# Two softmax attentions of a four-block network: where transposition, values and logits stand in a software-pipelined step

## The reference

```python
def fox_mixer(q, k, v, f_logit):          # 8 heads, in blocks of 128 queries
    ...
    logits = (einsum('bqhd,bshd->bhqs', qb, k) * scale
              + cq[..., None] - cum_k[:, :, None, :])
    p = masked_softmax(logits, causal)
    return einsum('bhqs,bshd->bqhd', p, v)

def dsa_mixer(q, ckv, k_rope, q_idx, k_idx, w_idx, w_uk, w_uv):   # 8 heads
    ...
    score = einsum('bqhs,bqh->bqs', relu(einsum('bqhd,bsd->bqhs', qi, k_idx)), wi)
    _, idx = top_k(score, n_keep)          # 128 keys for each query
    logits = (einsum('bqhr,bqkr->bqhk', qa, c_sel)
              + einsum('bqhe,bqke->bqhk', qr, kr_sel)) * scale
    p = masked_softmax(logits, valid)
    return einsum('bqhk,bqkr->bqhr', p, c_sel)
```

## Time and profile before

| | |
|---|---|
| median of 3 runs | 2276.22 us (2272.16 to 2279.46) |
| profiled execution: time, span | 2279.5 us, 2278.2 us |
| TensorE busy | 2219.5 us, 97% of the span |
| VectorE busy | 1348.9 us, 59% |
| ScalarE busy | 560.6 us, 25% |
| GpSimd busy | 192.0 us, 8% |
| mean granted TensorE clock | 0.995 of full speed |
| fox attention | from 131.8 to 258.2 us of the span |
| dsa attention | from 259.3 to 314.5 us |

### The profile page before, as it was taken

How to read it: one execution, slowest core, us unless ns; L and a number is a source line. 1 busy time by engine, 2 the same in 40 slices (tenths; PEclk the granted TensorE clock), 3 DMA queues, 4 the chain that set the end, 5 groups by cost and what they waited for, 6 DMA issues and landing times.

```text
span 2278.2 us, 29581 instructions
## 1 busy us (share of the span) xinstructions
PE 2219.5 (97%) x10992; PEld 1589.9 (70%) x10992; DVE 1348.9 (59%) x3440; ACT 560.6 (25%) x1421; POOL 192.0 (8%) x207
## 2 busy tenths in 40 slices
PE   9999999999999999999999999999999999999988
PEld 7776578888888885558888888888857534333333
DVE  6777757666566667876665666767786522222224
ACT  2223431101001206772110000333572111111110
POOL 0013430000000002330000000000020011111100
PEclk9999999999999999999999999999999999999999
DMA  5211032232222320002232222232205899999997
GB/s 211 75 57 47 13 123 77 90 93 85 82 93 91 116 74 19 1 1 67 82 93 90 78 92 93 75 103 64 66 9 232 326 422 422 424 422 424 424 423 305
DMA packets 60207, 346.54 MB, mean 152 GB/s; under 512 B 9248, under 2 KB 10144, under 8 KB 42208
## 3 DMA queue, kind: packets, MB, share of 16 engines
q1 hardware_dynamic: 55360, 335.03, 39.6%
q0 software_dynamic: 3840, 6.46, 0.8%
q10 hardware_dynamic: 864, 3.15, 0.3%
HBM read 337.59 MB, written 17.30 MB: 156 GB/s over the span
## 4 chain that ended last, share of the span: by engine, by line
PE 87%; DMA 7%; DVE 4%; ACT 1%; issue 1%; SPq 0%; DVEq 0%; POOLq 0%; ACTq 0%
PE bank L632 30%; PE bank L638 8%; PE bank L645 8%; PE bank L653 8%; DMA places<-in_experts 7%; PE bank L3038 6%; PE bank L3046 3%; PE bank L621 3%; PE bank L1098 2%; PE bank L1083 2%; PE bank L1110 2%; PE bank L2998 1%; PE bank L727 1%; PE bank L3011 1%; PE bank L1305 1%
## 5 line engine op out<-in xcount | busy, mean ns | idle before, releaser
L3038 PE MATMUL bank<-places,xT 128*64 128x512 f32 x824 | 183.8, 594 | 13.5 <-DMA places<-in_experts 13.4
L3245 DVE TENSOR_SCALAR square<-bank,mt 128x256 f32<-128x256 f32 x32 | 15.5, 483 | 287.2 <-ACT rope L3150 287.2
L3038 PEld LDWEIGHTS bank<-places,xT 128*64 128x64 f32 x824 | 59.4, 137 | 132.3 <-issue 118.0
L1959 DVE TENSOR_TENSOR third<-first,bank 128x256 f32<-128x256 f32 x106 | 44.7, 421 | 151.0 <-PE bank L632 150.3
L632 PE MATMUL bank<-u,ring 128*128 128x256 f32 x540 | 130.3, 381 | 1.1 <-DVE y_ab L1993 1.1
L632 PE MATMUL bank<-h,ring 128*128 128x256 f32 x512 | 121.0, 379 | 0.0
L632 PE MATMUL bank<-h_sums,w_sum 128*128 128x256 f32 x512 | 120.9, 379 | 0.0
L632 PEld LDWEIGHTS bank<-u,ring 128*128 128x128 f32 x540 | 101.2, 190 | 17.8 <-issue 3.3
L632 PE MATMUL bank<-u_mlp_sums,w_sum 128*128 128x256 f32 x480 | 113.4, 379 | 0.0
L632 PE MATMUL bank<-u_mlp,ring 128*128 128x256 f32 x480 | 113.4, 379 | 0.0
L2650 POOL TENSOR_SCALAR exps<-exps,small,gates 128x128 f32<-128x128 f32 (+1 forms) x64 | 56.4, 882 | 660.9 <-DVE small L2444 660.9
(11 more groups left out here) (558 smaller groups left out, 4415.2 us busy)
## 6 DMA issues: line engine op xcount, KB each, us to landing
places<-in_experts SPq DMA_DIRECT2D x56, 2048.0 KB, 35.3
ring<-in_dense SPq DMA_DIRECT2D x216, 512.0 KB, 4.2
places<-in_experts SPq DMA_DIRECT2D x40, 1024.0 KB, 24.6
x<-in_experts SPq DMA_DIRECT2D x12, 1024.0 KB, 37.3
w<-in_experts SPq DMA_DIRECT2D x10, 1024.0 KB, 31.3
consts<-in_experts SPq DMA_DIRECT2D x10, 1024.0 KB, 32.0
x<-in_experts SPq DMA_DIRECT2D x4, 2048.0 KB, 32.8
consts<-in_consts SPq DMA_DIRECT2D x1, 2310.5 KB, 16.6
```

Of the source, the lines that this page charges most:

```text
L3038: ins = k.pe.matmul(bank[a * CAP:(a + 1) * CAP, :], xT[:, kk % 4, kk // 4, :], w[:, (2 * (kk % 2) + a) * EH:(2 * (kk % 2) + a + 1) * EH], ...
```

## The change

It only moves code. In a fox step TensorE does the first half of the transposition ahead of the logits. In a dsa step TensorE does transposition(n-3), then values(n-4), then logits(n), and the keep-busy matmuls come behind these; ScalarE copies the transposed weights ahead of the exps; VectorE copies them ahead of the masks.

```diff
 def pe_fox_step(k, n):
+    if 0 <= n - 2 < len(FOX):
+        pe_fox_turn(k, n - 2, 0)
     if n < len(FOX):
         pe_fox_logits(k, n)
-    if 0 <= n - 2 < len(FOX):
-        pe_fox_turn(k, n - 2, 0)
     if 0 <= n - 3 < len(FOX):
         pe_soft_values(k, n - 3, k.ch7)
...
     for step in range(len(FOX), len(SOFT) + 4):
+        if len(FOX) <= step - TURN_LAG < len(SOFT):
+            pe_soft_turn(k, step - TURN_LAG)
+        if len(FOX) <= step - TURN_LAG - 1 < len(SOFT):
+            pe_soft_values(k, step - TURN_LAG - 1, k.ch6)
         if step < len(SOFT):
             pe_soft_logits(k, step)
...
         if step >= len(SOFT):
             pe.wait_ge(s["masked"], 2 * min(step - 1, len(SOFT)))
             pe_keep(k, logits_bank(k, step, 0), 4)
-        if len(FOX) <= step - TURN_LAG < len(SOFT):
-            pe_soft_turn(k, step - TURN_LAG)
-        if len(FOX) <= step - TURN_LAG - 1 < len(SOFT):
-            pe_soft_values(k, step - TURN_LAG - 1, k.ch6)
...
-        if step < len(SOFT):
-            act_exps(k, step, SOFT[step][2], "masked", "exp_done", sized_tile)
         n = step - TURN_LAG
         if len(FOX) <= n < len(SOFT):
             w = P * (SOFT[n][2] + 1)
             soft_valued(k, act, n - 2)
             act.wait_ge(s["t_done"], 2 * n + 1)
             act.copy(k.ETs[n % 2][0][:, 0:w], k.bank[4][:, 0:w]).then_inc(s["turned0"], 1)
+        if step < len(SOFT):
+            act_exps(k, step, SOFT[step][2], "masked", "exp_done", sized_tile)
...
+        if len(FOX) <= step - TURN_LAG < len(SOFT):
+            dve_soft_turned(k, step - TURN_LAG)
         if step < len(SOFT):
             kind, m, b = SOFT[step]
...
-        if len(FOX) <= step - TURN_LAG < len(SOFT):
-            dve_soft_turned(k, step - TURN_LAG)
```

## The result

| us | before | with the change |
|---|---|---|
| median of 5 runs each | 2276.22 | 2291.64 |
| lowest and highest | 2272.16 to 2279.46 | 2288.86 to 2292.96 |
| profiled execution, its span | 2279.5, 2278.2 | 2291.79, 2290.4 |
| ratio, 95% interval | | 1.0069, 1.0058 to 1.0080 |

The account below looks back on a forecast made before the run. TensorE, nearly always at work in both attentions, was taken as the bound. Order terms 1.25 + 2.0 + 5.7 = 9.0 us plus 3.4 us of clock gave 12.4, added to the 2276.2 median: 2288.6 us, range 2280 to 2297.

Parts of the forecast that it names:

- Fox beside the projection: Fox attention up to TensorE's restart at 215.13: late logits pass their delay on through VectorE, 1.25 us more.
- step 10 pays about 0.4 for the same wait as step 4: Fox step 10: the transposition waits for GpSimd's weighting as in step 4, about 0.4 us, an estimate.
- The saving by shape: Fox steps: transposes behind dense work or other transposes, not logits, save 0.15 us for the change of tile shape.
- The end at 0 for V's change of shape: Fox steps: if values behind logits paid nothing for the shape change, another 1 us gained over eight steps.
- Fox behind the projection: Fox steps 13 to 15: transposition halves sharing one bank wait for it to be emptied, 2.0 us more.
- Dsa: Dsa attention: values at three changes of head wait for ScalarE's store behind the exps, 7.9 against 2.2 us, 5.7 more.
- the signs named beforehand: Profile after: waits of 2.4 to 3.1 us at V(20), V(24), V(28); dsa stage 5 to 6 us longer without clock.
- Clock: Dsa attention: one more 6.8 us stretch at half clock than before, 3.4 us; ends -3.4 and +6.8.
- rival B: Dsa attention: a half-clock stretch behind each change of head, 2292.0 us, or 2295 with another elsewhere; chance 0.25.
- Rival A: Same waits, no added half-clock stretch, 2285.2 us, or 2281.8 if the one of before goes; lower case 0.13.
- Rival C: Faster: waits before T(21) and T(25) go, shape saves in 13 fox steps, clock stays up; 2268.6 us, chance 0.04.
- Rival D: Fox waits hidden by VectorE's stretches, only the dsa term holds; 2285.3 us, chance within the forecast's share.

Follow-up runs that it names:

- e11: e10 with the first half of the transposition ahead of the logits in fox steps 3, 6, 7, 8 and 9; 2271.58 us, ratio 0.9984.
- e1: The kernel before with only the change's fox part, dsa steps as before on every engine; 2281.13 us, ratio 1.0030.
- e4: The kernel before with only ScalarE's dsa order changed: copy of the transposed weights, then store, then exps; 2272.05 us, ratio 0.9988.
- e5: The kernel before with only TensorE's dsa order of the change (transposition, values, logits); 2307.89 us, one run.
- e3: The whole change with ScalarE's store also moved ahead of the exps of its step; 2287.95 us, ratio 1.0062.
- e8: e1 with the transposition first only in fox steps 0 to 11, beside the projection; 2277.79 us, ratio 1.0020.
- e9: e1 with the second halves of the transposition, from step 10's on, in a bank of their own; 2279.92 us, ratio 1.0018.
- e6: The kernel before with only the copies of the transposed weights moved first on ScalarE and VectorE in the dsa steps; 2284.17 us, ratio 1.0043.
- e2: The kernel before with only the change's dsa part, fox steps as before; 2286.99 us, ratio 1.0056.
- e7: The whole change with seven small constant matmuls on TensorE ahead of V(20), V(24) and V(28); 2283.53 us, ratio 1.0038.
- e10: e4 with the two banks of e9 for the transposition behind the projection; 2271.06 us, ratio 0.9980.

## Why the prediction was right, and where its sizes were off

Predicted 2288.6 us within 2280 to 2297, slower; measured 2291.6. The sum for the profiled execution was 12.4 us, and it came to 12.2; that agreement is luck, as the terms show. At the medians, where 12.4 was carried over, it is 15.4.

**Fox beside the projection: predicted 1.25, measured 2.0.** The wait of step 4 is there (1.05 us against 0.9, ended by GpSimd), L(4) is 1.57 us late and not 1.3, and 1.50 instead of 1.25 us arrive at line 517. Steps 7, 8 and 9 save 0.15 us each, as put. The step that failed is "step 10 pays about 0.4 for the same wait as step 4": with the saving of 0.15 it was put at 0.25 net, and it costs 0.75 (197.93 to 202.73 before, 197.19 to 202.74 after). Its wait is 0.69 us, and not for GpSimd but for ScalarE's copy, which stands behind exps of step 9. I had looked at when the weights are ready, and not at the queue of the engine that copies them. Step 11 pays 0.2, as put: 1.50 - 0.45 + 0.75 + 0.22 = 2.0.

The saving by shape held: fox step 9 takes 4.33 us (190.59 to 194.92), before 4.48 (191.18 to 195.66). It isn't all in T, though: four transposes take 0.53 us there and not 4 x 0.11, and the dense group in front of them takes 1.73 instead of 1.83. V behind L costs what V behind T did, as I had kept it. The end at 0 for V's change of shape is out. The weight loads of step 9 show where the 0.15 us lie, before and then after:

```profile
194.27 0.42 PEld L830 LDWEIGHTS bank<-consts,y_ab 128*128 128x128 f32 x4 [0.33 <-issue]
```

```profile
192.10 0.57 PEld L830 LDWEIGHTS bank<-consts,y_ab 128*128 128x128 f32 x4
```

Behind logits the first load starts together with the first transpose (194.27); behind dense work it starts 0.22 us ahead of it (192.10, and the transposes at 192.32).

The Trainium skill ("TensorE: Matmul & The Clock Gate", section "Step-by-step: what each phase is for") has weights loaded ahead, into a background buffer or where row groups don't conflict; if that held everywhere, no step would get shorter. Here it holds where transposes follow dense work and not where they follow logits: the loads of step 9 above, its 0.15 us, and the 0.46 us of e11 over three steps show that a part of a load is exposed at the change of shape.

**Fox behind the projection: predicted 2.0, measured 2.0.** It is read best in e1, which has no half clock there: 44.1 us from restart to V(15) against 42.1 (217.00 to 261.07, 215.13 to 257.23). Step 14 of before, from its first transposition to the dense group behind its values, and then of e1:

```profile
227.06 0.60 PE L830 MATMUL bank<-consts,exps_fox 128*128 128x128 f32 x4
...
230.56 1.12 PE L727 MATMUL bank<-y_ab,consts 128*128 128x512 f32 x2
```

```profile
229.62 0.60 PE L830 MATMUL bank<-consts,exps_fox 128*128 128x128 f32 x4
230.96 0.33 PE L830 MATMUL bank<-consts,y_ab 128*128 128x128 f32 x1 [0.73 <-ACT o_tokens L1556]
...
233.93 1.13 PE L727 MATMUL bank<-y_ab,consts 128*128 128x512 f32 x2
```

3.50 us became 4.31, 0.81 more where 0.98 - 0.15 = 0.83 was worked out. In the same way step 13 pays 0.69 (0.72) and step 15 0.48 (0.49), together 1.98. This term held place by place. The 3.7 us of the change between restart and V(15) have 1.7 of clock on top, from the stretch at 215.58; e4 and e5, with the fox order of before, have such a stretch too, and e1 hasn't, so it isn't the change's work.

**Dsa: predicted 5.7, measured 4.7.** The mechanism was the one predicted: V(20), V(24) and V(28) wait for the store, which stands behind two exps, whose L is last in its step. It was right in place and in who ends the wait. Waits of 2.7, 2.1 and 2.1 were predicted at 3.1, 2.4 and 2.4. The chain was sized nearly right: from the end of L(27), where T(25) starts (299.81), to V(24) (302.75) it takes 2.94 us against 3.0, in front of V(28) 2.98, in front of V(20) 3.52 against 3.7 (283.75 to 287.27). The term that was mis-sized is what TensorE does in it: I had put T at 0.59, the distance to a V that follows at once, and before a wait its two halves are busy for 0.41 us each, 0.82 in all. Of the signs named beforehand two fell short here: the stage is 4.7 us longer without the clock, not 5 to 6, and the waits run from 2.1 to 2.7 us, not from 2.4 to 3.1. e3 adds that the store alone isn't the bound: once it is out of the way, GpSimd is.

**Clock: predicted 3.4, measured more.** The stage has 20.5 us at half clock against 6.8, 6.8 us of time, so rival B (a stretch behind each change of head) is what the profile shows here, and its 2292.0 us is the figure nearest to the median. In the profiled pair 5.0 us came back elsewhere, where before happened to have 10.2 us of half clock and after 3.4. That isn't the change's work: it is why the sum of one pair fitted. Nor has before's profiled execution two stretches, as I had it, but four, of 3.4, 6.8, 6.8 and 7.1 us, the last at its very end. Over all runs the granted clock gives it better. Twice the missing share of the clock, times the span, is the half-clock time of an execution: 13.6 to 15.2 us on average for before, in each comparison, 30 us for the change. Half of the difference, some 8 us, is clock, and the other 8 order. The clock's term should have been about 8, order's 8 where I had 9.0. This split is an estimate, good to 1 or 2 us: the half clock at the very end of an execution (7.1 us in the profiled one of before, 2.9 in that of after) is counted in it, and TensorE has hardly any work there.

Rival A (no added stretch) fell; of what spoke for it, the wait at 215.13 that no stretch follows, the change, e8 and e9 have the opposite, a stretch of 3.4 us from 215.6, 214.7 and 215.1 on. Rival C (the early copies pay) is out as the change stands, but its idea was half right: on ScalarE, with the store along, the early copy pays (e4). Rival D fell: both fox terms hold.

Open is why e1, with the dsa order untouched, had 10.2 us at half clock in that stage, and e6 17.1 with waits of only 0.5 to 1.6 us. Their averages over all runs are 20.5 and 32.0 us. Waits bring such stretches, but the profile of one execution doesn't tell which wait brings which.

## What to carry to other kernels

Where an operation is last in its step, count what lies between it and the next operation that needs its chain's end; a copy-out that stands behind the same chain on another engine, though its data are long ready, turns that distance into a wait. Move the copies whose data are ready ahead of the chain and leave the bound engine's order alone: that gained here (e4, with T's copy and the store moved together), where moving TensorE's work lost. On an engine where such a copy would have to wait for its data, moving it ahead holds up the chain itself (VectorE in e6). Next to a wait of 2 us look for what the clock does behind it, for it may cost as much again.

## What the runs showed of the hardware

- The granted clock fell to 0.50, for 3.4 to 10.2 us at a time, in the change, behind waits of only 1.6 to 2.2 us among small matmuls. It is plainest in e2: V(20), V(24) and V(28) start at 281.65, 295.57 and 309.74 behind waits of 2.15, 1.64 and 1.83 us, and a stretch of 3.4 us at half clock starts at 283.85, 297.50 and 311.15. Seven small matmuls in each of three waits (e7) took all of them from the stage of the change: 20.5 us at half clock to none.
- The spread between runs of one kernel is mostly this. The runs of before in the comparisons lie at 2271 to 2283 us, with standard deviations of 2.3 to 2.7 us; with half the half-clock time taken off each, 1.2 to 1.4 us are left, and the averages of before lie at 2267.7 to 2268.1. By the same measure the change is at 2275.9, e2 at 2272.6, e1 at 2272.1, e4 at 2266.8 and e10 at 2266.0. The clock is recorded to three digits, one of which is worth 2.3 us here, so these averages hold to some tenths at best.
- Four transposes take 0.15 us longer behind logits, where the tile shape changes, than among dense matmuls, and a fox step gets 0.15 us shorter when they move to the dense side. Values pay the same behind logits as behind transposes (0.37 us from start to start in both versions, 180.71 to 181.08 after).
